# First layer without the multiplication by ones, one instruction for the negated maximum of the mixture heads, and softmax reciprocals moved to GpSimd

## What is computed

```python
def blocked_attention(q, k, v, scale):
    ...
        s = jnp.einsum('bhgqd,bhkd->bhgqk', qblk, k, preferred_element_type=jnp.float32) * scale
        p = jax.nn.softmax(s, axis=-1)
        return jnp.einsum('bhgqk,bhkd->bhgqd', p.astype(v.dtype), v)

for l in range(DEPTH):
    mod = (c_act @ w_ada[l] + b_ada[l])[:, None, :]
    sh_a, sc_a, g_a, sh_m, sc_m, g_m = jnp.split(mod, 6, axis=-1)
    h = x * (1.0 + sc_a) + sh_a
    proj = h @ w_in[l]
    ...
    y = jnp.concatenate([heads_to_seq(y_a), heads_to_seq(y_b), heads_to_seq(y_c)], -1) @ w_o[l]
    x = layer_norm(ALPHA * x + (1.0 + g_a) * y, ln1_g[l], ln1_b[l])
    h = x * (1.0 + sc_m) + sh_m
    y = jnp.square(jax.nn.relu(h @ w1[l])) @ w2[l]
    x = layer_norm(ALPHA * x + (1.0 + g_m) * y, ln2_g[l], ln2_b[l])
```

## Time and profile before

| | before |
|---|---|
| median of 3 runs | 1468.88 us |
| lowest and highest run | 1468.24 us, 1470.12 us |
| span of the profiled execution | 1470.4 us |
| mean granted TensorE clock | 0.965 |
| attention, first norm to last norm, first layer | 188.6 to 320.2 us |
| the same, second layer | 896.7 to 1027.4 us |

### The profile page before, as it was taken

The page is one execution under the profiler, slowest core; times in us unless marked ns, Lnnn a source line. Parts: engine busy times, 40 slices in busy tenths (PEclk is TensorE's granted clock), DMA queues, the critical chain, the costliest instruction groups (busy, mean ns, idle before and its releaser), DMA issues.

```text
span 1470.4 us, 19994 instructions
## 1 busy us (share of the span) xinstructions
PE 1340.6 (91%) x6696; PEld 1119.5 (76%) x6696; DVE 1027.5 (70%) x1794; ACT 598.7 (41%) x1212; POOL 292.1 (20%) x312
## 2 busy tenths in 40 slices
PE   4998988799899999999969999879989999999992
PEld 2897866687788787888759977768778888888882
DVE  6667799877678554645795878989684855444478
ACT  0356478661532222221244547878152232222221
POOL 0031075220116000000230404723010700000025
PEclk9998999899999999999989999989999999999996
DMA  8854600004333332434236462010423333333331
GB/s 291 305 184 158 222 21 14 26 7 137 101 126 125 116 127 86 127 123 150 81 114 211 154 219 88 1 39 1 143 79 101 94 93 97 95 93 99 94 100 57
DMA packets 87867, 165.44 MB, mean 113 GB/s; under 512 B 7992, under 2 KB 18616, under 8 KB 87792
## 3 DMA queue, kind: packets, MB, share of 16 engines
q1 hardware_dynamic: 87264, 162.39, 34.2%
q10 hardware_dynamic: 528, 2.10, 0.4%
HBM read 160.26 MB, written 4.19 MB: 112 GB/s over the span
## 4 chain that ended last, share of the span: by engine, by line
PE 62%; DVE 20%; DMA 6%; ACT 4%; issue 4%; POOL 3%; SPq 0%; DVEq 0%; ACTq 0%; POOLq 0%
PE bank L1311 20%; PE bank L1313 20%; PE bank L1312 20%; DMA slab_raw<-in_w_in 2%; DMA ada_w<-in_w_ada 2%; DVE ada_sum L822 2%; DVE pt_lo L1062 2%; DVE smax L1049 2%; DVE k_lo L1020 1%; PE bank L1340 1%; POOL prob L455 1%; DVE prob L1042 1%; DVE X L1090 1%; DVE stats L1093 1%; DVE tmp L1087 1%
## 5 line engine op out<-in xcount | busy, mean ns | idle before, releaser
L1311 PE MATMUL bank<-hT_hi,slab_hi 128*128 128x512 f32 x576 | 225.1, 391 | 0.4 <-ACT kB L642 0.4
L1312 PE MATMUL bank<-hT_lo,slab_hi 128*128 128x512 f32 x576 | 224.4, 390 | 0.0
L1313 PE MATMUL bank<-hT_hi,slab_lo 128*128 128x512 f32 x576 | 224.3, 389 | 0.0
L1142 DVE TENSOR_TENSOR slab_lo<-slab_raw,slab_hi 128x512 fp32r<-128x512 f32 x240 | 182.6, 813 | 58.9 <-ACT slab_hi L776 51.4
L1311 PE MATMUL bank<-slab_hi,h_hi 128*128 128x512 f32 x512 | 203.0, 397 | 2.9 <-ACT mod_a L793 2.1
L1312 PE MATMUL bank<-slab_lo,h_hi 128*128 128x512 f32 x512 | 202.3, 395 | 0.0
L1313 PE MATMUL bank<-slab_hi,h_lo 128*128 128x512 f32 x512 | 202.1, 395 | 0.0
L1311 PE MATMUL bank<-slab_hi,hT_hi 128*128 128x384 f32 (+3 forms) x448 | 151.8, 339 | 6.3 <-DVE slab_lo L866 3.3
L1312 PE MATMUL bank<-slab_lo,hT_hi 128*128 128x384 f32 (+3 forms) x448 | 150.9, 337 | 0.0
L1313 PE MATMUL bank<-slab_hi,hT_lo 128*128 128x384 f32 (+3 forms) x448 | 150.9, 337 | 0.0
L822 DVE SCALAR_TENSOR_TENSOR ada_sum<-ada_w,c_col,ada_sum 128x512 f32<-128x512 f32 x168 | 129.1, 769 | 20.2 <-DMA ada_w<-in_w_ada 17.1
(11 more groups left out here) (197 smaller groups left out, 2584.1 us busy)
## 6 DMA issues: line engine op xcount, KB each, us to landing
slab_raw<-in_w SPq DMA_DIRECT2D x256, 256.0 KB, 2.7
ada_w<-in_w_ada SPq DMA_DIRECT2D x48, 1024.0 KB, 6.3
slab_raw<-in_w_in SPq DMA_DIRECT2D x48, 192.0 KB, 5.2
slab_raw<-in_w_o SPq DMA_DIRECT2D x32, 256.0 KB, 3.1
slab_raw<-in_w_in SPq DMA_DIRECT2D x16, 256.0 KB, 4.9
band<-bias_rows SPq DMA_DIRECT2D x8, 448.0 KB, 3.1
slab_raw<-in_w_in SPq DMA_DIRECT2D x16, 144.0 KB, 4.4
X<-in_x SPq DMA_DIRECT2D x1, 2048.0 KB, 10.1
```

The costliest lines, as they stand in the source:

```text
L1142: dve.tensor_tensor(slab_lo[:, slot, :], slab_raw[:, slot, :], f32(slab_hi[:, slot, :]), ALU.subtract).then_inc(slab_lo_done, 1)
L1311: pe.matmul(dst, a_hi, w_hi, start=first, stop=False)
L1312: pe.matmul(dst, a_hi, w_lo, start=False, stop=False)
L1313: return pe.matmul(dst, a_lo, w_hi, start=False, stop=last)
```

## The change

Three edits, in both layers except where it says otherwise.

1. In the first layer SP no longer loads `lnx_g` and `lnx_b`, and POOL makes no affine piece; it raises `x_ready` by four before the attention.
2. On A heads the fused instruction now gives -(score + band) and takes the minimum of it, which is the negated maximum. It writes `smax[...,0]` itself and signals `maxed`; the wait on itself and the multiplication by -1 are gone. ACT's exponential reads the negated scores with scale -1.
3. The reciprocal of a unit's row sum is made by POOL, as a power of -1 on 128x1 elements, with a wait for `exped` before it and a wait on itself behind it, for every unit without an affine piece: all 64 of the first layer, and 48 of the second. For the sixteen units with one (8 to 23 of the second layer) it stays on DVE.

```diff
+def affine_unit(l, u):
+    return l > 0 and AFFINE_FROM <= u < AFFINE_FROM + 4 * TT
...
@@ SP @@
-                        sp.dma_start(lnx_g[:, :], t_in["ln_rows"][l, 0:1, :].broadcast_to([P, D])).then_inc(lnx_in, 16)
-                        sp.dma_start(lnx_b[:, :], t_in["ln_rows"][l, 1:2, :].broadcast_to([P, D])).then_inc(lnx_in, 16)
+                        if l > 0:
+                            sp.dma_start(lnx_g[:, :], t_in["ln_rows"][l, 0:1, :].broadcast_to([P, D])
+                                         ).then_inc(lnx_in, 16)
+                            sp.dma_start(lnx_b[:, :], t_in["ln_rows"][l, 1:2, :].broadcast_to([P, D])
+                                         ).then_inc(lnx_in, 16)
@@ POOL @@
+            pool.memset(mone[:, :], -1.0).then_inc(setup_pool, 1)
...
+                if l == 0:
+                    pool.sem_inc(x_ready, TT)
                 for u in range(UNITS):
-                    wait_apart(pool, summed, l * UNITS + u + 1)
                     p = prob[:, u % 4, :]
+                    if affine_unit(l, u):
+                        pool.wait_ge(summed, sums_by_dve(l, u) + 1)
+                    else:
+                        pool.wait_ge(exped, l * UNITS + u + 1)
+                        after(step(pool.tensor_tensor(smax[:, u % 4, 2:3], smax[:, u % 4, 1:2], mone[:, 0:1], ALU.pow)))
                     pool.tensor_scalar(p, p, smax[:, u % 4, 2:3], 1.0, ALU.mult, ALU.mult).then_inc(normed, 1)
-                    if u == AFFINE_FROM:
+                    if l > 0 and u == AFFINE_FROM:
                         pool.wait_ge(bank_ready, l * B_LAYER + 8)
-                        pool.wait_ge(lnx_in, l * 32 + 32)
-                    if AFFINE_FROM <= u < AFFINE_FROM + 4 * TT:
+                        pool.wait_ge(lnx_in, 32)
+                    if affine_unit(l, u):
                         n = u - AFFINE_FROM
                         affine_part(n // 4, n % 4, lnx_g, lnx_b)
@@ ACT @@
                         act.activation(prob[:, s % 4, :], src, ACT.Exp, bias=smax[:, s % 4, 0:1],
-                                       accum_out=smax[:, s % 4, 1:2]).then_inc(exped, 1)
+                                       scale=-1.0 if m == "A" else 1.0, accum_out=smax[:, s % 4, 1:2]
+                                       ).then_inc(exped, 1)
@@ DVE @@
-                            step(dve.tensor_tensor_reduce(prob[:, s % 4, :], bank[s % 3][:, :],
-                                                          band[:, 384 - P * qt:896 - P * qt], 1.0, -3.0e38,
-                                                          ALU.add, ALU.max, smax[:, s % 4, 3:4]))
-                            settle()
-                            dve.tensor_scalar(smax[:, s % 4, 0:1], smax[:, s % 4, 3:4], -1.0, None, ALU.mult
-                                              ).then_inc(maxed, 1)
+                            dve.tensor_tensor_reduce(prob[:, s % 4, :], bank[s % 3][:, :],
+                                                     band[:, 384 - P * qt:896 - P * qt], -1.0, 3.0e38,
+                                                     ALU.add, ALU.min, smax[:, s % 4, 0:1]).then_inc(maxed, 1)
...
                     u = s - 1
-                    if 0 <= u < UNITS:
+                    if 0 <= u < UNITS and affine_unit(l, u):
                         dve.wait_ge(exped, l * UNITS + u + 1)
```

21 lines of the change are left out of this document (10 added, 11 removed).

## The result

| | before | after |
|---|---|---|
| median | 1468.56 us (4 runs) | 1448.09 us (4 runs) |
| lowest and highest run | 1465.03, 1470.12 us | 1447.62, 1450.06 us |
| span of the profiled execution | 1470.4 us | 1446.6 us |

The account below looks back on a forecast made before the run. POOL's pieces were taken to bound layer one's units 9 to 26, bias loads the A heads. Savings of 6.5 plus twice 4.1, minus 0.3, make 14.4: span 1470.4 becomes 1456.0, median 1454.5 us, range 1449.5 to 1462.

Parts of the forecast that it names:

- the rest is shifted and neither gains nor loses: Behind the attention, loads of `w_o` follow PE's own progress, so those stretches were to change by nothing.
- Term 1: First layer, units 9 to 26: without affine pieces the window falls from 34.87 to 28.4 us, -6.5 us (5.2 to 7.8).
- the two are level: C heads: DVE needs 6.3 us a head against PE's 6.36, so whatever else delays either one shows.
- Term 2: Reciprocals off DVE, 0.07 us a unit: per layer 0.3 in units 1 to 9, 0.4 in 26 to 32, 0.8 in B heads.
- The price on POOL: Power, wait and norm take 1.32 us a unit, hidden below PE's 1.59; 0.3 us charged at layer two's last piece.
- the chain gets no longer: From exponential to norm: POOL's power starts right after the exponential, while the reciprocal waited on DVE behind the next maximum.
- Term 3: A heads: shorter way from accumulator read to `pt_lo` and earlier bias load, -2.6 us a layer (1.6 to 3.2).
- 0.20 us off each unit: A heads: without multiplication, wait and reciprocal, accumulator read to `pt_lo` falls from 0.28 to 0.08 us.
- one of four savings is lost: Heads A1 to A3: the last unit waits for a cooled PE, so the saving is 0.8 + 3 x 0.6 = 2.6 us.
- What is moved gives nothing: Rival: DVE and POOL hinder each other or DVE merely idles longer, leaving 6.2 us of gain, 1462.7 us; chance 0.13.
- The slower rival: In the attention POOL's cycle of power and norm, 2.22 us, becomes the bound, giving 1479 us; chance 0.04.
- the one in which the time comes back: Rival: the attention gains, but a hidden wait (ACT's key copies, bias loads) takes it all, within 3 us; chance 0.03.

Follow-up runs that it names:

- negmax_only: Only the negated maximum from one DVE instruction (edit 2), against the kernel before at its old addresses: 1464.23 us, ratio 0.9966.

## Why the prediction was right or wrong

**"Behind the attention ... the rest is shifted and neither gains nor loses."** This step failed, and it is worth 9.7 us, half of the result. The argument looked for waits and loads that come earlier. It looked at `mone` only for its `memset`, and not at what its 32 bytes do to the tiles behind it. All of it lies in one group of matmuls, whose distance fell from 0.234 to 0.227 us. The padding alone reproduces it and the old addresses take it away. The trace of before could have told me to ask, since the same matmul took 391 ns in the first product and 397 in the second, but nothing in it says which address is the fast one.

**Term 1, -6.5 us forecast, -3.8 measured.** The mechanism was right: POOL was the bound and no longer is; a query instruction among the former pieces takes 0.69 us as against 1.88. The floor was mis-sized. The failed step is "the two are level" with DVE's 6.3 us for a C head, which then was to fall to 6.0. It was summed from the smallest distances of the earlier trace rows, and left out `v_lo`. DVE's timeline in the changed kernel, in the window of units 9 to 26 (start, duration, instruction):

```profile
205.55 0.68 DVE L1063 TENSOR_REDUCE smax<-bank 128x1 f32<-128x512 f32 x1
206.26 0.69 DVE L1076 TENSOR_TENSOR pt_lo<-bank,pt_hi 128x512 fp32r<-128x512 f32 x1
206.99 0.69 DVE L1044 TENSOR_TENSOR q_hi<-qC,q_hi 64x512 fp32r<-64x512 f32 x1
207.70 0.69 DVE L1063 TENSOR_REDUCE smax<-bank 128x1 f32<-128x512 f32 x1
208.31 0.68 DVE L1076 TENSOR_TENSOR pt_lo<-bank,pt_hi 128x512 fp32r<-128x512 f32 x1
208.91 0.68 DVE L1063 TENSOR_REDUCE smax<-bank 128x1 f32<-128x512 f32 x1
209.73 0.69 DVE L1076 TENSOR_TENSOR pt_lo<-bank,pt_hi 128x512 fp32r<-128x512 f32 x1
210.45 0.68 DVE L1084 TENSOR_TENSOR hT_lo<-bank,hT_hi 64x512 fp32r<-64x512 f32 x1
211.17 0.69 DVE L1063 TENSOR_REDUCE smax<-bank 128x1 f32<-128x512 f32 x1
```

DVE has no idle time in these 5.62 us, and its instructions follow each other at 0.60, but just as often at 0.71 to 0.73, and once at 0.82. Three units with one query part and one `hT_lo` take 5.62; with a fourth unit of at least 1.20 (0.60 + 0.60) and one of some 1.33 (a middling 0.61 + 0.72) the head is 6.8 to 7.0 us, not 6.0, and above PE's 6.36. For 4.25 heads (17 units) 6.95 gives 29.5, and with the 1.4 us of new keys 30.9, near the window's 31.06. So DVE bounds it: in the whole window it waits 0.7 us for other engines, and PE's longest waits (up to 1.3 us) end with DVE's `pt_lo`. The higher end of my own bounds, at the rate of units 26 to 32, gave 29.6; I had chosen the middle by PE's floor.

**Term 2, 0.07 us a unit.** The failed step is "where DVE leads, a reciprocal costs 0.07". In layer one's units 9 to 26, from the start of a maximum to that of the following `pt_lo` it is 0.72 us on average with the reciprocal between them and 0.69 without it. The 0.07 was mostly time in which `pt_lo` began late anyway; 0.03 a unit was left, and 0.14 for the window of edit 1. Units 26 to 32, forecast at -0.4 a layer, came out at -0.07 in layer one; the +0.18 of layer two is -0.07 as well, and 0.25 that belong to POOL (below). The start, forecast at -0.3 a layer, can't be claimed; alone edit 3 made it 0.6 to 0.8 longer, and the change 0.5 and 0.2 as a mean. So of 3.0 us forecast for the reciprocals in both layers the change shows 0.4.

Only the B heads gave the number that was forecast, 0.8 in edit 3 alone (0.67 and 0.34 as means over the change), and that was partly luck. Their units with a `k_lo` or `q_lo` fell from 2.00 to 1.80 us; 0.07 of the 0.20 is the reciprocal, the other 0.13 is that DVE's instruction itself got shorter: before, it began 0.3 us ahead of the end of a norm on POOL, now 0.2 us at most and mostly 0.1. In the A heads of the kernel before, such instructions took 0.68 to 0.69 us where no norm ran beside them and 0.70 to 0.82 where one did. One of them before, and in the changed kernel:

```profile
293.02 0.81 DVE L1027 TENSOR_TENSOR q_lo<-qB,q_hi 96x512 fp32r<-96x512 f32 x1
...
282.18 0.68 DVE L1044 TENSOR_TENSOR q_lo<-qB,q_hi 96x512 fp32r<-96x512 f32 x1
```

And 1.84 us was no floor of PE: with edit 3 the window runs at 26.89 / 15 = 1.79 us a unit.

**The price on POOL: hidden.** Right for the steady part: powers at a median of 0.55 us, up to 1.00, and PE's waits for the norm are few. The 0.3 us charged for the last piece of layer two were right too. They show in the window behind, units 26 to 32, which takes 11.98 us where pieces come before it (layer two of the change, both layers of edit 3 alone) and 11.73 where none do. In layer two of the changed kernel, the last piece on POOL, the late power and norm, PE's wait for that norm, and the window:

```profile
923.47 1.28 POOL L447 TENSOR_TENSOR X<-X,lnx_b 128x512 f32<-128x512 f32 x1
924.71 1.00 POOL L473 TENSOR_TENSOR smax<-smax,mone 128x1 f32<-128x1 f32 x1
925.81 0.69 POOL L474 TENSOR_SCALAR prob<-prob,smax 128x512 f32<-128x512 f32 x1
...
926.55 0.66 PE L1492 MATMUL bank<-ident,prob 128*128 128x128 f32 x4 [1.17 <-POOL prob L474]
...
925.32:937.30 11.98, 9.69 (x72) 8.50 (x72) 11.30 (x18) 9.87 (x23) 8.80 (x15) 1.00 0.00 1
```

At the line of the transposes all waits of PE for the norm come to 4.1 us, 9.4 before:

```profile
L1492 PE MATMUL bank<-ident,prob 128*128 128x128 f32 x512 | 81.7, 284 | 8.1 <-POOL prob L474 4.1 <-DVE pt_lo L1076 3.3
```

The sentence "the chain gets no longer" fails at the start at most, where the pipeline isn't full and nothing lies between exponential and norm; what shows there goes together with the clock.

**Term 3, -2.6 us a layer forecast, -3.3 measured** (3.4 and 3.2 from the means; 3.5 with edit 2 alone). The term is the step that was mis-sized, in two of its parts: "0.20 us off each unit" and "one of four savings is lost". The start distances of an A unit's instructions in `negmax_only`:

```profile
256.40 0.08 DVE L1043 DVE_READ_ACCUMULATOR2_ANT smax<- 128x1 f32 x1
256.40 0.16 DVE L1054 RECIPROCAL smax<-smax 128x1 f32<-128x1 f32 x1
256.48 0.67 DVE L1060 TENSOR_TENSOR pt_lo<-bank,pt_hi 128x512 fp32r<-128x512 f32 x1
```

And in the changed kernel:

```profile
264.62 0.08 DVE L1059 DVE_READ_ACCUMULATOR2_ANT smax<- 128x1 f32 x1
264.62 0.69 DVE L1076 TENSOR_TENSOR pt_lo<-bank,pt_hi 128x512 fp32r<-128x512 f32 x1
```

Edit 2 alone takes the way from accumulator read to `pt_lo` from 0.28 us to 0.08: the next instruction no longer waits behind the read but starts with it. I had given these 0.20 to edits 2 and 3 together. Both together take 0.28, and the second units of the heads show it: 2.33 us before, 2.13 with edit 2, 2.05 in the change.

Second, "one of four savings is lost" to the cold PE. Here the third unit decides, and it goes by when the granted clock falls from 2.4 to 1.2 GHz. In `negmax_only` the clock was full (0.98 to 1.00) during the second unit of all eight heads, and each third unit took 1.27 or 1.28 us. In the kernel before it took 1.47 or 1.48 where the clock was still full and 1.72 to 1.83 where it had fallen. In four profiles of the change the third unit takes 1.21 to 1.25 us where the second had a clock of 0.98 to 1.00, and 1.34 to 1.97 where it had already fallen (0.65 to 0.95). So the loss exists, but not in each head, and it falls on the third unit. Why the clock falls earlier in some heads no run shows.

The wait for the bias stayed, as forecast: 3.9 to 4.9 us from the last maximum of a head to the first of the next, 4.2 on average, as against 4.0 to 5.0 and 4.3.

**The sum.** Attention alone: forecast 14.4; by the windows 10.6, by the runs with old addresses 12.5 (9.1 to 15.9, from the ratio) or 14.7 (the medians 1454.74 and 1469.48). Term 1 was 2.7 too large, term 2 2.6 too large, term 3 1.4 too small over both layers, and the price on POOL came out within 0.1: 14.4 - 2.7 - 2.6 + 1.4 + 0.1 = 10.6. Then came 9.7 that I had not asked about. The 1.5 us between span and median, which the forecast carried over, change nothing in the sum, but they are not a property of the kernel: after the change the profiled execution took 1448.38 us with a span of 1446.6, so there the time lies above the span. The profiled execution of before took 3.0 us more than that of after ahead of the attention, where the change does nothing.

**The rivals.** "What is moved gives nothing" came near for edit 3, whose reciprocals are worth 2.1 us alone and nothing visible in the A heads on top of edit 2, but its reason hardly occurred: instructions on DVE did not get slower beside POOL, except for one `q_hi` right behind the pieces (0.94 us in layer two). DVE's query and key instructions even got shorter in the A heads (0.73 to 0.68 us on average) and the B heads (0.81 to 0.68). DVE's `q_hi` in the rows above takes 0.69 us while a power on POOL begins beside it. POOL pays instead: in its timeline the power that begins at 205.08, while DVE makes a `k_lo` from two tiles (204.94 to 205.63), takes 0.96 us, and the one that begins during a maximum, which reads a bank, 0.55. Of the 112 powers all that met no `k_lo`, `q_hi`, `q_lo` or `v_lo` on DVE (two tiles in each) took 0.54 to 0.55 us.

```profile
205.08 0.96 POOL L473 TENSOR_TENSOR smax<-smax,mone 128x1 f32<-128x1 f32 x1 [1.24 <-ACT prob L716]
206.14 0.69 POOL L474 TENSOR_SCALAR prob<-prob,smax 128x512 f32<-128x512 f32 x1
...
209.29 0.55 POOL L473 TENSOR_TENSOR smax<-smax,mone 128x1 f32<-128x1 f32 x1 [0.42 <-ACT prob L716]
```

The Trainium skill (Perfetto Trace Analysis, Optimizing Scalar/DVE Operations) says that offloading between DVE and GpSimd might not help. The measurement neither refutes nor quite bears out that: edit 3 alone gives a ratio of 0.9983 (0.997 to 0.9996), a small gain, whose interval just leaves out 1, and no loss. The slower rival and the one in which the time comes back did not occur.

## What to carry to other kernels

Before you forecast that a part of a kernel "only shifts", list the tiles whose addresses the edit moves, and after the run compare the distance of the same matmul in stages that the edit didn't touch. A floor for an engine is to be taken from its mean distances over a whole head, with the waits in them, and not from the smallest ones; here DVE, which I had called level with PE, was the bound. A 128x1 instruction in front of one that begins late anyway is worth less than its own distance (0.03 of 0.07 us in the C heads), and all of it where nothing waits (0.08 in the second units of the A heads). And look for a price in the window behind the one in which it arises.

## What the runs showed of the hardware that was not expected

- A stream of fp32 matmuls of 128x512 with one stationary tile each follows at 0.227 us where the stationary and the moving tile lie a multiple of 256 bytes apart (remainders 0 and 256 of 512), and at 0.232 to 0.234 where they don't (480, 32, 64, 128). Over 1536 matmuls that is 9.7 us. It depends on the distance, not on either address. A change of it was seen in the second MLP product only: the scores of the attention (`k_hi` moving, `q_hi` stationary, a multiple of 512 apart in every kernel here) stay at 0.233 all the same, so the distance is not the only thing that costs those 6 ns.
- An unused tile of 32 bytes made the kernel before 0.7% faster (0.9932).
- On DVE, an instruction that waited for the accumulator's result by a semaphore began 0.12 us after the read and took its own time after it; the 0.20 us vanish as a whole when the result is final in the first instruction.
- The power of -1 on 128x1 elements takes POOL 0.55 us, and 0.55 to 1.00 us beside an instruction of DVE with two inputs from the tiles. Such an instruction of DVE pays too when it begins 0.3 us ahead of the end of POOL's norm: 0.81 us in place of 0.68.
- The same edit can lengthen a stretch at one granted clock and shorten it at another: POOL's reciprocals made the start of the attention 0.4 to 0.6 us longer at 0.71 to 0.76, and 0.2 us shorter at 0.91 to 0.97.
